# Attention's second product in three fp32r passes; first taps and the scan's product on GpSimd, the scan and the division in other places on VectorE

## The reference, cut to what matters

```python
z = h @ w_in[i]
q, k, v, xr, yr, ga, gr = jnp.split(z, split_points, axis=-1)
...
logits = jnp.einsum('bnqhgd,bnkhd->bnhgqk', qb, kb) * (HEAD_DIM ** -0.5)   # banded, |i-j| <= 128
probs = jax.nn.softmax(jnp.concatenate([logits, sink_col], axis=-1), axis=-1)[..., :-1]
out = jnp.einsum('bnhgqk,bnkhd->bnqhgd', probs.astype(v.dtype), vb)
...
xf = directional_conv(xr, rnn_conv_w[i, 0], rnn_conv_b[i, 0], False)       # width 4, and xb backwards
gate_a = jax.nn.sigmoid(xb @ w_a + b_a); gate_x = jax.nn.sigmoid(xb @ w_x + b_x)   # in 4 blocks of 256
a = jnp.exp(log_a); mult = jnp.sqrt(-jnp.expm1(2.0 * log_a))               # mult is 1 at the start
u = x * gate_x * mult                                                      # then a linear scan over time
...
merged = sigmoid(ga) * (attn @ w_proj_attn[i]) + sigmoid(gr) * (rnn @ w_proj_rnn[i])
```

## Time and profile before

| | |
|---|---|
| median of 3 runs | 949.04 us (949.01 to 949.27) |
| profiled execution | 949.1 us, its span 947.3 us |
| granted TensorE clock, mean | 0.997 |
| busy over the span: TensorE, VectorE, ScalarE, GpSimd | 98%, 77%, 61%, 0% |

### The profile page before, as it was taken

One profiled execution on the slowest core, in us unless ns is written; L12 is line 12 of the kernel. 1 busy time (PEld: TensorE's weight loads), 2 busy tenths in 40 slices (PEclk: granted clock), 3 DMA queues, 4 the chain that ended last, 5 costly groups with the idle time before them and its releaser, 6 DMA issues.

```text
span 947.3 us, 12574 instructions
## 1 busy us (share of the span) xinstructions
PE 927.0 (98%) x5100; PEld 800.1 (84%) x5100; DVE 729.6 (77%) x981; ACT 577.1 (61%) x730; POOL 1.4 (0%) x9
## 2 busy tenths in 40 slices
PE   5999999999999999999999999999999999999996
PEld 3898988988888888888889889888888888888885
DVE  5888898787867867767868698888878676866755
ACT  4578899764356644555345889987435564545540
POOL 0000000000000000000000000000000000000000
PEclk9999999999999999999999999999999999999998
DMA  9546444584485555566443644456656656555521
GB/s 333 153 163 200 136 156 157 185 305 164 156 266 182 199 198 178 192 203 204 160 161 119 211 159 155 134 180 197 256 179 217 226 187 205 186 180 198 201 89 45
DMA packets 118457, 174.62 MB, mean 184 GB/s; under 512 B 3968, under 2 KB 78976, under 8 KB 117888
## 3 DMA queue, kind: packets, MB, share of 16 engines
q1 hardware_dynamic: 118256, 173.79, 55.0%
q10 hardware_dynamic: 144, 0.03, 0.0%
HBM read 172.76 MB, written 1.05 MB: 183 GB/s over the span
## 4 chain that ended last, share of the span: by engine, by line
PE 88%; DVE 7%; ACT 4%; DMA 0%; issue 0%; DVEq 0%; ACTq 0%
PE ring L548 13%; PE ring L550 13%; PE ring L549 13%; PE ring L601 9%; PE ring L597 9%; PE misc L548 5%; PE misc L549 5%; PE misc L550 5%; PE ring L600 5%; PE ring L598 5%; PE misc L778 2%; DVE sb_w_lo L1253 2%; PE ring L721 1%; PE misc L837 1%; ACT sb_w_hi L933 1%; DVE sb_tmp L1485 1%
## 5 line engine op out<-in xcount | busy, mean ns | idle before, releaser
L1253 DVE TENSOR_TENSOR sb_w_lo<-sb_raw,sb_w_hi 128x2048 fp32r<-128x2048 f32 x138 | 294.8, 2148 | 65.8 <-ACT sb_w_hi L933 65.8
L933 ACT CAST sb_w_hi<-sb_raw 128x2048 fp32r<-128x2048 f32 x138 | 246.3, 1796 | 19.6 <-DMA sb_raw<-in_w_out_dram 4.3
L601 PE MATMUL ring<-sb_x_both,sb_w_hi 128*128 128x512 f32 x272 | 107.6, 396 | 0.0
L597 PE MATMUL ring<-sb_x_both,sb_w_hi 128*128 128x512 f32 x272 | 107.5, 395 | 0.0
L548 PE MATMUL ring<-sb_w_hi,sb_x_both 128*128 128x512 f32 x272 | 107.1, 394 | 0.0
L549 PE MATMUL ring<-sb_w_lo,sb_x_both 128*128 128x512 f32 x272 | 106.0, 390 | 0.0
L550 PE MATMUL ring<-sb_w_hi,sb_x_both 128*128 128x512 f32 x272 | 106.0, 390 | 0.0
L600 PE MATMUL ring<-sb_x_both,sb_w_lo 128*128 128x256 f32 x272 | 75.7, 278 | 0.0
L598 PE MATMUL ring<-sb_x_both,sb_w_lo 128*128 128x256 f32 x272 | 75.4, 277 | 0.0
L548 PE MATMUL ring<-sb_x_both,sb_w_hi 128*128 128x256 f32 x256 | 72.6, 284 | 0.0
L550 PE MATMUL ring<-sb_x_both,sb_w_lo 128*128 128x256 f32 x256 | 72.4, 283 | 0.0
(11 more groups left out here) (229 smaller groups left out, 2111.8 us busy)
## 6 DMA issues: line engine op xcount, KB each, us to landing
sb_raw<-in_w_in_dram SPq DMA_DIRECT2D x40, 1024.0 KB, 5.3
sb_raw<-in_w_up_dram SPq DMA_DIRECT2D x34, 1024.0 KB, 5.2
sb_raw<-in_w_down_dram SPq DMA_DIRECT2D x18, 1024.0 KB, 5.0
sb_raw<-in_w_proj_attn_dram SPq DMA_DIRECT2D x8, 1024.0 KB, 5.2
sb_raw<-in_w_proj_rnn_dram SPq DMA_DIRECT2D x8, 1024.0 KB, 5.1
sb_hb<-in_w_up_dram SPq DMA_DIRECT2D x8, 1024.0 KB, 5.3
sb_raw<-in_w_out_dram SPq DMA_DIRECT2D x6, 1024.0 KB, 6.2
sb_raw<-in_w_ple_gate_dram SPq DMA_DIRECT2D x6, 1024.0 KB, 5.4
```

Source lines behind the costliest of these rows:

```text
L597: nc.tensor.matmul(bank_of(*key), hi[:, cols], x_both[:, k], start=k == 0, stop=False)
L601: last = nc.tensor.matmul(bank_of(*key), hi[:, cols], x_both[:, k + 1], start=False, stop=k + 2 == KT)
L933: nc.scalar.copy(hi_at[home][:, at], raw_at[home][:, at]).then_inc(s_hi_part, 1)
L1253: nc.vector.tensor_tensor(lo_at[home][:, 0:size], raw_at[home][:, 0:size], hi_at[home][:, 0:size].bitcast(F32), ALU.subtract).then_inc(s_s ...
```

## The change

- `mix_values` multiplies high and low parts of v and of the probabilities in three fp32r passes instead of one float32 product. `probs_back` now writes the high part (`p_hi`, in `pT`'s place); VectorE takes the low part from PSUM (`probs_low`, into the place of q's first four turned heads). ScalarE rounds v once in a layer (step 2) and VectorE takes its low part in place (`v_low`, step 3). The scores' product stays as it was.
- `conv_base` moves from ScalarE to GpSimd, and so do the two memsets and the product ahead of a scan (`scan_input`).
- On VectorE, the scan of a pair of steps is done one step later, after the first `split_to` of steps 2, 4, 6 and, for the last, after step 7. The division of rounds 1 and 3 stands ahead of the first `split_to` of steps 4 and 6; that of rounds 0 and 2 stays behind it.
- On ScalarE, `probs_back` stands ahead of `split_to(name, 1)` instead of behind it.

```diff
--- before.py
+++ after.py
@@ -236,11 +236,11 @@
 STATS_DONE = ((2, LN_STEPS + 2), (2 * LN_STEPS + 2, 3 * LN_STEPS + 2))
 
 PER = dict(
-    qk_lo_ready=5, ln_step=2 * TT * LN_STEPS, ln_norm=4 * TT, x_turned=3 * 4, x_hi=3 * 4, x_ready=3 * 4,
+    qk_lo_ready=5, probs_lo=ROUNDS, v_ready=1, v_hi=1, ln_step=2 * TT * LN_STEPS, ln_norm=4 * TT, x_turned=3 * 4, x_hi=3 * 4, x_ready=3 * 4,
     rope_step=6, qk_turned=5, qk_ready=5,
     scores=ROUNDS, soft_step=6 * ROUNDS, exp_done=5 * ROUNDS, probs=ROUNDS, probs_turned=ROUNDS,
     probs_back=ROUNDS, mixed=ROUNDS, attn_hi=ROUNDS, attn_ready=ROUNDS,
-    param_step=16, param_exp=1, conv_base=8, conv_step=48, rin_hi=8, rin_ready=8,
+    param_step=16, param_exp=1, conv_base=16, conv_step=48, rin_hi=8, rin_ready=8,
     decay=16, pair_ready=8, m2_done=8, gated=8, root=GROUPS, rg_step=3 * GROUPS, scanned=GROUPS,
     rnn_step=4, yr_gelu=1, rnn_hi=2, rnn_ready=2, merge=4, p_turned=1, p_hi=1, p_ready=1,
     taken=24, gate_base=12, tap_step=36, gelu=12, hidden=12, f_hi=12, f_ready=12, added=2 * TT, ple_step=2,
@@ -282,9 +282,12 @@
 
         h = sb("h", [P, TT, D])
         lnp = sb("lnp", [P, 2, D])
-        qk = sb("qk", [P, TT, QK_HEADS, HEAD_DIM])
-        v = sb("v", [P, TT, KV_HEADS, HEAD_DIM])
-        qkT = sb("qkT", [P, QK_HEADS, SEQ], F32R)
+        qk, at = sb_at("qk", [P, TT, QK_HEADS, HEAD_DIM])
+        v_hi = again("v_hi", [P, TT, KV_HEADS, HEAD_DIM], F32R, at + 4 * KT * SEQ)
+        v, at = sb_at("v", [P, TT, KV_HEADS, HEAD_DIM])
+        v_lo = again("v_lo", [P, TT, KV_HEADS, HEAD_DIM], F32R, at)
+        qkT, at = sb_at("qkT", [P, QK_HEADS, SEQ], F32R)
+        p_lo = again("p_lo", [P, TT, GROUP, P], F32R, at)
         yg = qk[:, :, :, :].rearrange("p t h d -> p (t h d)")[:, 0:KT * SEQ].rearrange(
             "p (k s) -> p k s", k=KT)
         hf = lnp[:, :, :].rearrange("p i (k s) -> p (i k) s", s=SEQ)
@@ -294,7 +297,8 @@
         ga = sb("ga", [P, TT, D])
         gr = xT[:, :, :].rearrange("p (t a) s -> p t (a s)", t=TT)
         soft = sb("soft", [P, GROUP, SEQ])
-        pT = sb("pT", [P, TT, GROUP, P])
+        pT, at = sb_at("pT", [P, TT, GROUP, P])
+        p_hi = again("p_hi", [P, TT, GROUP, P], F32R, at)
         scan_in, at = sb_at("scan_in", [P, 2, 4, SEQ])
         decay_a, root_m = scan_in[:, 0], scan_in[:, 1]
         scan_hi = again("scan_hi", [P, 2 * 4 * SEQ], F32R, at)
...
@@ -540,6 +547,39 @@
             nc.gpsimd.affine_select(out=masks[:, 1, :], in_=masks[:, 1, :], compare_op=ALU.is_ge, fill=MASKED,
                                     base=0, pattern=[[1, P]], channel_multiplier=-1).then_inc(s_const, 1)
 
+            def conv_base(l, i):
+
+                direction, b = divmod(i, RNN_BLOCKS)
+                if i == 0:
+                    pool.wait_ge(s_small, 32 * l + 32)
+                xr = (l, f"xr{b // 2}", b % 2)
+                pool.wait_ge(s_emptied[RING[xr][0]], read_out(*xr))
+                pool.wait_ge(s_gated, value("gated", l, max(0, i - 1)))
+                for j in range(2):
+                    ft = 2 * b + j
+                    nc.gpsimd.tensor_scalar(xc[:, i % 2, j, :], xT[:, ft, :], rnnp[:, direction, ft, 0:1],
+                                            rnnp[:, direction, ft, 4:5], ALU.mult, ALU.add).then_inc(s_conv_base, 1)
+
+            def scan_input(l, g):
+
+                direction, c = divmod(g, 2)
+                state = (hb if direction else hf)[:, 4 * c:4 * c + 4, :]
+                first = SEQ - 1 if direction else 0
+                pool.wait_ge(s_root, value("root", l, g + 1))
+                nc.gpsimd.memset(root_m[:, :, first:first + 1], 0.5).then_inc(s_rg_step, 1)
+                nc.gpsimd.memset(decay_a[:, :, first:first + 1], 0.0).then_inc(s_rg_step, 1)
+                pool.wait_ge(s_rg_step, value("rg_step", l, 3 * g + 2))
+                nc.gpsimd.tensor_tensor(state, state, root_m[:, :, :], ALU.mult).then_inc(s_rg_step, 1)
+
+            for l in range(DEPTH):
+                for i in range(3):
+                    conv_base(l, i)
+                for i in range(1, 2 * RNN_BLOCKS):
+                    if i + 2 < 2 * RNN_BLOCKS:
+                        conv_base(l, i + 2)
+                    if i % 2 == 1:
+                        scan_input(l, i // 2)
+
 
         @block.tensor
         def _(pe):
@@ -832,10 +872,11 @@
 
             def mix_values(l, r):
 
-                pe.wait_ge(s_probs_back, value("probs_back", l, r + 1))
+                pe.wait_ge(s_v_ready, value("v_ready", l, 1))
+                pe.wait_ge(s_probs_lo, value("probs_lo", l, r + 1))
                 for kb in range(TT):
-                    last = nc.tensor.matmul(misc[:, 2, :], v[:, kb, r // TT, :], pT[:, kb, :, :],
-                                            start=kb == 0, stop=kb == TT - 1)
+                    last = three(misc[:, 2, :], [x[:, kb, r // TT, :] for x in (v_hi, v_lo)],
+                                 [p_hi[:, kb, :, :], p_lo[:, kb, :, :]], kb == 0, kb == TT - 1)
                 last.then_inc(s_mixed, 1)
 
 
@@ -958,20 +999,6 @@
                 act.wait_ge(s_products, PRODUCT[l, name, part])
                 nc.scalar.activation(dst, bank_of(*key), func, scale=scale).then_inc(s_emptied[RING[key][0]], 1)
 
-            def conv_base(l, i):
-
-                direction, b = divmod(i, RNN_BLOCKS)
-                if i == 0:
-                    act.wait_ge(s_small, 32 * l + 32)
-                xr = (l, f"xr{b // 2}", b % 2)
-                act.wait_ge(s_emptied[RING[xr][0]], read_out(*xr))
-                act.wait_ge(s_gated, value("gated", l, max(0, i - 1)))
-                for j in range(2):
-                    ft = 2 * b + j
-                    last = nc.scalar.activation(xc[:, i % 2, j, :], xT[:, ft, :], ACT.Identity,
-                                                bias=rnnp[:, direction, ft, 4:5], scale=rnnp[:, direction, ft, 0:1])
-                last.then_inc(s_conv_base, 1)
-
             def conv_hi(l, i):
                 direction, b = divmod(i, RNN_BLOCKS)
                 act.wait_ge(s_conv_step, value("conv_step", l, 6 * (i + 1)))
@@ -1035,7 +1062,7 @@
 
             def probs_back(l, r):
                 act.wait_ge(s_probs_turned, value("probs_turned", l, r + 1))
-                nc.scalar.copy(pT[:, :, :, :].rearrange("p a g t -> p (a g t)"),
+                nc.scalar.copy(p_hi[:, :, :, :].rearrange("p a g t -> p (a g t)"),
                                misc[:, 2:4, :].rearrange("p a n -> p (a n)")).then_inc(s_probs_back, 1)
 
             def attn_out(l, r):
@@ -1141,11 +1168,9 @@
                 unit_out(l, "q1")
                 split_to(l, "xr0", 0)
                 xr_out(l, 0, 0)
-                conv_base(l, 0)
                 split_to(l, "xr0", 1)
                 xr_out(l, 0, 1)
                 conv_hi(l, 0)
-                conv_base(l, 1)
                 split_to(l, "xr1", 0)
                 xr_out(l, 1, 0)
                 conv_hi(l, 1)
@@ -1153,7 +1178,6 @@
                 gate_curves(l, 0)
                 split_to(l, "xr1", 1)
                 xr_out(l, 1, 1)
-                conv_base(l, 2)
                 for i, name in enumerate(WITH_BLOCK[1:], 1):
                     split_to(l, name, 0)
                     if i >= 4:
@@ -1166,15 +1190,16 @@
                     if name == "ga0":
                         qk_copies(l, range(4))
                     gate_curves(l, i)
+                    if 3 <= i <= 6:
+                        probs_back(l, i - 3)
                     split_to(l, name, 1)
                     if name == "kv":
                         unit_out(l, name)
-                    if i + 2 < 2 * RNN_BLOCKS:
-                        conv_base(l, i + 2)
                     if name == "ga0":
                         qk_copies(l, [4])
-                    if 3 <= i <= 6:
-                        probs_back(l, i - 3)
+                        all_emptied(act, l, [("kv", t) for t in range(TT)])
+                        nc.scalar.copy(v_hi[:, :, :, :].rearrange("p t h d -> p (t h d)"),
+                                       v[:, :, :, :].rearrange("p t h d -> p (t h d)")).then_inc(s_v_hi, 1)
                     if i % 2 == 1:
                         root(l, i // 2)
                     if name == "gr0":
@@ -1464,6 +1489,23 @@
                     last = nc.vector.tensor_scalar(soft[:, i, :], soft[:, i, :], sm[:, 5, i:i + 1], None, ALU.mult)
                 last.then_inc(s_probs, 1)
 
+            def v_low(l):
+                dve.wait_ge(s_v_hi, value("v_hi", l, 1))
+                nc.vector.tensor_tensor(v_lo[:, :, :, :].rearrange("p t h d -> p (t h d)"),
+                                        v[:, :, :, :].rearrange("p t h d -> p (t h d)"),
+                                        v_hi[:, :, :, :].rearrange("p t h d -> p (t h d)").bitcast(F32),
+                                        ALU.subtract).then_inc(s_v_ready, 1)
+
+            def probs_low(l, r):
+
```

(32 more changed lines are left out.)

## The result

The changed kernel takes 974.04 us (973.01 to 975.66, 4 runs) where the kernel before took 949.15 us (949.01 to 949.79, 4 runs) on the same chip: the ratio is 1.0263 [1.0249, 1.0277]. The profiled execution is the slowest of the four (975.66 us); it has a span of 973.6 us against 947.3, so 26.3 us have to be found. The mean granted clock of TensorE is 0.987 against 0.997.

What follows compares the result with a forecast made beforehand. The prediction took TensorE's own work (98% busy) as the bound, with 0.2 us of reserve on VectorE. Savings of 1.44 and 0.40 against waits of 2.4, 0.45 and 3.1 gave +8.2 us over two layers: 957.2 us, range 953 to 970.

Steps and rivals of the forecast that it cites:

- A: Mixer steps 4 to 6: only misplaced scans and the division's wait delay TensorE; 957.2 us, range 953 to 961, chance 0.45.
- The `ga1` wait: Step 4 of each layer: TensorE's 0.40 us wait for ScalarE's read-out of `ga1` goes.
- The wait of 0.45 for `gr0`: Step 6 gates: ScalarE reads `gr0` only after conv 7, so TensorE waits 0.45 us in each layer.
- Rival B: Convs beside GpSimd's product: it holds VectorE up, conv ends 2.3 us later; 969.0 us, chance 0.41 for all of B.
- The sum: Per layer: -1.44 - 0.40 + 2.4 + 0.45 + 3.1 = +4.1 us; two layers +8.2, giving 957.2 us.
- So its duration is not in the sum: GpSimd's product before the scans, taken as 2.4 us: hidden, adding nothing unless it slows VectorE's conv.
- The first taps are hidden: GpSimd's two first taps, 0.3 to 0.6 us each, run while VectorE waits or splits, due one split later.
- TensorE's saving: Probabilities by v: a round takes 1.36 us instead of 1.72, saving 1.44 us in a layer.
- C: Whole mixer: everything is hidden and only TensorE's saving of 3.7 us is left; 945.3 us, chance 0.07.
- D: TensorE's new waits: about half of those forecast, cancelling the gain; 949 us, chance 0.07.

Runs made afterwards that it cites:

- e3: The changed kernel with VectorE's scans and divisions back in their old places, GpSimd keeping first taps and products; 965.03 us, ratio 1.0171.
- e8: The changed kernel with VectorE's attention low part, scan, division before the split (steps 4, 6); GpSimd products only for scans 2 and 3, after their convs; 949.14 us.
- e12: e8 with the first taps of pair 4 back on ScalarE; 946.96 us, ratio 0.9976 against the kernel before.

## Why the prediction was wrong, point by point

- **The sign and the mechanism of A were right.** It forecast waits before the turns of rounds 1 and 3 for the attention's low part, 2.4 and 3.1 us. With the product out of the conv's way they measured 2.95 and 2.68; all new waits of a layer were forecast at 5.95 and the two make 5.63. VectorE stands 2.09 us ahead of division 1, as forecast (3.10 ahead of division 3), and ScalarE stood 3.10 us ahead of the decays of step 4 until the scan ended, as forecast. The `ga1` wait went from 0.40 to 0.23, not to nothing. The wait of 0.45 for `gr0` wasn't there without the lock.
- **Rival B happened, beside A.** The product took 2.43 us where nothing held it (forecast 2.4); it lengthened conv 3, 5 and 7 by 2.1 us each (forecast 2.3): 4.60, 4.59 and 4.59 us against 2.45. Before the turn of q and k 0.96 us were measured (forecast 1.3), before turn 1 4.58 (forecast 2.4 + 2.3), before `gr0`'s gates 2.21 (0.45 + 2.3), before turn 3 only 1.17 (3.1). B's waits were forecast at 11.85 us a layer and measured at 9.4: each wait is shorter where TensorE has already been held, so the chain was counted twice towards its end. I gave B 0.41 against 0.45 for A; the argument against it, that VectorE keeps its place until the conv is over, is what the trace refutes: of six operations that follow one another, the third lasts 2.62 us. A and B were weighed as rivals, and both happened.
- **The step that failed is "The sum".** It counts a wait as the time that TensorE stands, at full clock afterwards; the term for the clock is nothing, without a reason. The trace shows the clock at 0.50 for about five microseconds of work after the wait of 4.58 and for some three after the 2.21: about 8.0 us over the profiled execution. B as forecast (969.0), less 2 x 2.45 for the waits and plus 0.3 for the products, gives 964.4, inside the stated range; measured were 974.04, and 8.0 of the 9.6 us between them are the clock. The same term puts A's own case out of its range of 953 to 961: the run nearest to it, the product later, came to 967.27, of which the clock is about 6 us and the turn of q and k 1.9; without these two it is 959, inside that range.
- **A second step failed in the forecast of 957.2: "So its duration is not in the sum".** GpSimd's product was put at nothing there. With the products of scans 2 and 3 out of the convs' way, the time falls by 6.8 us (974.04 to 967.27), a part of it by the clock.
- **"The first taps are hidden" was wrong.** Priced at 0.3 to 0.6 each, they took 0.55 each (1.09 the pair) where undisturbed, which is right; but pair 4's take 3.50 beside a split. Alone this move costs 2.3 us (the ratio of 1.0024), and undoing it for pair 4 gains 2.2 (949.14 to 946.96).
- **TensorE's saving was right.** Six products start 0.23 us apart, from 119.71 to 120.41 for the first four, so a round takes 1.40 us; forecast was 1.36.
- **Rivals C and D didn't happen.** Both needed waits of half of A's or less, and the waits came to more than A's.

The Trainium skill's rule that I weighed in B (SBUF — State Buffer, Who interferes with whom), that the second to issue waits for the whole of the first, holds in both directions here: the third operation of conv 5 was held by the product (2.62 us instead of 0.48), and a tap by the split (2.66 us instead of 0.55). Its price for the product, by half of the 4497 ns for 2048 columns (GPSIMD Engine Reference, Elementwise — side-by-side cycle accounting), is an estimate of 2.25 us; the trace has 2.43.

**What stays open.** The clock didn't fall after every wait. The order of before with GpSimd (`e3`) waits 2.40 us before turn 1 in both layers, from 129.4 to 131.8 and from 598.3 to 600.7. In layer 0 the clock stays at 1.00, in layer 1 it falls:

```profile
130.00:132.50 2.50, 0.68 (x7) 0.71 (x8) 2.50 (x7) 2.47 (x6) 0.00 (x0) 1.00 0.68 210
132.50:135.00 2.50, 2.50 (x20) 2.37 (x19) 2.50 (x4) 2.41 (x3) 0.82 (x1) 1.00 0.00 0
...
600.00:602.50 2.50, 1.85 (x13) 1.88 (x14) 2.50 (x4) 2.37 (x5) 0.00 (x0) 0.83 0.51 177
602.50:605.00 2.50, 2.50 (x12) 2.31 (x11) 2.48 (x4) 2.50 (x4) 1.39 (x2) 0.50 0.00 0
```

So two waits of one length in the same execution were followed by different clocks, and the length alone doesn't tell which one the clock answers to. In all the traces it fell behind every wait of the mixer of 2.68 us or more and behind each of 2.21; of those of 2.40 and of 1.85 it fell behind one in two, and never behind one of 1.25 or less. In `e8` and `e12`, where no wait of the mixer is over 0.7 us, the mean is 0.998 and 0.997. What the clock costs is worked out from the granted clock of the windows and seen in the pace of the 24 products; no run removed it alone.

Open too is which engine gets its turn. In conv 5 the product is recorded 0.37 us ahead of the operation that it holds (119.72 and 120.09). In `e8` the tap is recorded 0.39 us ahead of the split (96.38 and 96.77), and there the split goes first and holds the tap. No run separates the two cases.

## What to carry to other kernels

Where one engine is busy 98% of the time, look for the reserve at the place where it waits next for each of the others (here 0.2 us) before anything is moved into their queues; and price a wait of about two microseconds or more in TensorE's stream with the slower stretch that can follow it: here 8.0 us for 18.0 of new waits. Work given to GpSimd that reads SBUF was free here only where the VectorE instructions beside it don't read two SBUF tensors, and what GpSimd is held by counts too: the same two instructions took 1.09 or 3.50 us. And causes that delay the same instruction are to be forecast together, as a case of their own, and not as rivals: 19.2 and 13.3 us alone were 22.4 together.

## What the runs showed of the hardware

- A GpSimd instruction that reads SBUF can get its turn between two VectorE instructions that follow one another without a gap, and then holds the next one with two SBUF inputs to its own end: a conv of six took 4.59 us instead of 2.45 beside a product of 2.72, one of its operations taking 2.62. Beside two GpSimd operations of 1.53 us together it took 3.15, each of them holding one of its operations for 0.35. Five memsets of 2.86 us together held nothing.
- The reverse holds too, and there GpSimd didn't get its turn: beside a VectorE split of 2.3 us a pair of 128x256 operations took 3.50 us instead of 1.09, one of the two taking 2.66 (changed kernel) or 2.96 us (`e8`) instead of 0.55.
- Even an operation of 128x4 is held (0.68 us instead of 0.16), if it reads two SBUF tensors.
- TensorE's granted clock fell to 0.50 behind waits of 1.85 to 4.6 us, in kernels that are 96 to 97% busy, and stood there for five microseconds of work after the wait of 4.58. After one wait of 1.85 and two of 2.40 it did not fall.
